# Half of the token projections and of the convolution move from the first block into the gathers' block

## What is computed

```python
xn = rms_norm(h, norm1_g);  proj = xn @ w_in                 # 2560 columns
q, k, v, ga, gg = split(proj)                                # each 512 wide
# 4 heads: differential attention, ALiBi bias, causal, then rms_norm over a head's 128 columns
attn_out = diff_attention(q, k, v, lam, ...)
# 512 channels: u = ga*sigmoid(gg); causal depthwise conv of 31 taps; LayerNorm over groups of 64; silu
conv_out = conformer_conv(ga, gg, conv_w, conv_b, gn_g, gn_b)
h = h + concat([attn_out, conv_out]) @ w_out
# experts: per token 8 heads x top 16 of 128*128 keys; every chosen expert is one row of peer_u and one of peer_v
xn2 = rms_norm(h, norm2_g);  q = xn2 @ wq                    # 8 heads x 256
e, gate = product_key_top16(q, subkeys)
w = gate * gelu(sum_d(u_tab[e] * xn2));   h = h + sum_k(w * v_tab[e])
out = rms_norm(h, final_norm_g)[16:]
```

## Time and profile before

| | us |
|---|---|
| median of 3 runs (3079.91 to 3081.95) | 3081.67 |
| the profiled execution | 3080.33 |
| its span, first to last instruction | 3078.6 |
| mean granted TensorE clock | 0.856 |

### The profile page before, as it was taken

One profiled execution on the slowest core, in us unless ns is written; L12 is line 12 of the kernel. 1 busy time (PEld: TensorE's weight loads), 2 busy tenths in 40 slices (PEclk: granted clock), 3 DMA queues, 4 the chain that ended last, 5 costly groups with the idle time before them and its releaser, 6 DMA issues.

```text
span 3078.6 us, 35490 instructions
## 1 busy us (share of the span) xinstructions
PE 2300.7 (75%) x11776; PEld 848.3 (28%) x11776; DVE 2071.3 (67%) x4903; ACT 1328.8 (43%) x3979; POOL 1162.7 (38%) x1077
## 2 busy tenths in 40 slices
PE   9998857778677777777677777777777777777665
PEld 5555532222222222222222222222222222222211
DVE  3997426666677777777666666666666667666664
ACT  1023523444355555455544444444444444444443
POOL 1001004444354444445444344434444344444442
PEclk9999978898889898889898789878887788887886
DMA  5002139999999999999999999999999999999997
GB/s 215 21 28 73 58 125 415 426 426 427 426 422 426 412 424 416 420 415 426 427 421 426 426 427 426 426 427 423 422 426 425 424 423 425 427 427 421 424 426 310
DMA packets 165608, 1139.68 MB, mean 370 GB/s; under 512 B 18608, under 2 KB 21040, under 8 KB 32688
## 3 DMA queue, kind: packets, MB, share of 16 engines
q0 software_dynamic: 150096, 1082.80, 83.9%
q1 hardware_dynamic: 15328, 54.62, 4.6%
HBM read 1122.06 MB, written 15.28 MB: 369 GB/s over the span
## 4 chain that ended last, share of the span: by engine, by line
DMA 43%; PE 23%; ACT 10%; DVE 6%; issue 3%; POOL 1%; SPq 0%; DVEq 0%; POOLq 0%; ACTq 0%
DMA ring<-table,e_odd 21%; DMA ring<-table,e_even 20%; PE acc L1623 14%; PE qq_ps L1597 5%; DVE ring L1426 4%; ACT diag L1191 2%; ACT weight L1184 2%; ACT L1258 2%; ACT L1177 1%; PE proj L1570 1%; ACT gelu L1258 1%; ACT wide L1215 1%; PE acc L1661 1%; DVE wide L1441 1%; PE s_ps L1614 1%
## 5 line engine op out<-in xcount | busy, mean ns | idle before, releaser
L1623 PE MATMUL acc<-ring,diag 64*64 64x512 f32 x8192 | 1327.4, 734 | 695.0 <-ACT diag L1191 693.3
L1426 DVE CUSTOM_DVE_ANT_0 ring<-ring,xn_odd 128x1024 f32<-128x1024 f32 x512 | 626.7, 1224 | 366.8 <-DMA ring<-table,e_even 183.2
L1040 POOL DMA_INDIRECT ring<-table,e_even x512 | 567.2, 1108 | 791.2 <-PE acc L1623 700.9
L1426 DVE CUSTOM_DVE_ANT_0 ring<-ring,xn_even 128x1024 f32<-128x1024 f32 x512 | 626.4, 1223 | 337.7 <-DMA ring<-table,e_odd 168.7
L1040 POOL DMA_INDIRECT ring<-table,e_odd x512 | 568.1, 1110 | 706.7 <-PE acc L1623 665.3
L1258 ACT ACTIVATE gelu<-dots 128x1 f32<-128x1 f32 x1024 | 205.5, 201 | 1197.0 <-DVE dots L1426 1195.2
L1623 PEld LDWEIGHTS acc<-ring,diag 64*64 64x64 f32 x8192 | 250.0, 150 | 1469.2 <-ACT diag L1191 1342.0
L1191 ACT ACTIVATE diag<-pairs,weight 128x64 f32<-128x64 f32 x1024 | 356.0, 348 | 33.6
L1597 PE MATMUL qq_ps<-wq_rest,xnT_cur 128*128 128x256 f32 x896 | 262.6, 430 | 0.0
L1597 PEld LDWEIGHTS qq_ps<-wq_rest,xnT_cur 128*128 128x128 f32 x896 | 173.1, 209 | 174.1 <-issue 154.0
L1184 ACT ACTIVATE weight<-gelu,gate_even 128x1 f32<-128x1 f32 x512 | 150.7, 294 | 16.7
(11 more groups left out here) (237 smaller groups left out, 2106.3 us busy)
## 6 DMA issues: line engine op xcount, KB each, us to landing
ring<-table,e_even POOLq DMA_INDIRECT x512, 15.1
ring<-table,e_odd POOLq DMA_INDIRECT x512, 15.1
wq_rest<-wq SPq DMA_DIRECT2D x7, 1024.0 KB, 13.0
w_own<-w_units SPq DMA_DIRECT2D x10, 512.0 KB, 3.4
xT<-xt SPq DMA_DIRECT2D x8, 520.0 KB, 7.6
h_next<-x SPq DMA_DIRECT2D x8, 512.0 KB, 8.1
wide<-w_out SPq DMA_DIRECT2D x2, 2048.0 KB, 8.5
wide<-w_out SPq DMA_DIRECT2D x1, 4096.0 KB, 17.5
```

The costliest lines, as they stand in the source:

```text
L1040: pool.indirect_dma_start(out=ring[:, g % RING, :], out_offset=None, in_=table[:, :], in_offset=bass.IndirectOffsetOnAxis(ap=e_row[m % 2][ ...
L1426: dve.tensor_tensor_reduce(ring[:, g % RING, 0:D], ring[:, g % RING, 0:D], xn[(m // PH) % 2][:], 1.0, 0.0, ALU.mult, ALU.add, dots[:, k:k ...
L1623: ins = pe.matmul(acc[ACC_OF[t]][ROWS[j], HALF[i]], diag[ROWS[i], g % DIAGS, :], ring[ROWS[i], g % RING, D + j * 512:D + (j + 1) * 512], s ...
```

## The change

The first block now projects and convolves only the first 528 positions (`FRONT`: meta tokens and early tiles), in two segments of 264. The other 512 positions stay as raw transposed tokens in `x2`, normalised in the first block (`normalise_late`). Their projections become 20 jobs in the gathers' block, one a step from frame -7 (`FIRST_JOB`) to 12: SP loads the job's 512 KB of weights into the one buffer `w_job`, PE makes it in eight pieces in slots 6 to 13, ACT (for A units DVE) takes it out of PSUM in slot 14, SP stores keys, queries and values. The convolution of 512 tokens of one channel unit follows its A job: one tap a slot for 31 slots, then mean, variance, root, four part reciprocals, product, silu, store. Group means' matrix and the last 30 convolution inputs of the early half go through DRAM. Late attention moves back by 32 slots (`FRAME0` = 174), the order of output projections becomes 2, 3, 1, 4. Two pairs of expert heads (4, 5 and 6, 7) share two query-weight buffers: six reloads of 1 MB (`next_pair`), and from step 24 heads 4 and 5 lie in what was `x2` (two more). The first normalisation waits for `g2_row` alone.

```diff
-SEGS = [(0, 352), (352, 352), (704, 336)]
+FRONT = META + P * EARLY
+BACK = P * LATE
+SEGS = [(0, FRONT // 2), (FRONT // 2, FRONT // 2)]
...
-        FILLERS = [(Q[1], 0), (Q[1], 1), (K[2], 0), (K[2], 1), (K[2], 2), (Q[2], 0), (Q[2], 1), (K[3], 0), (K[3], 1),
-                   (K[3], 2), (Q[3], 0), (Q[3], 1), (Q[1], 2), (Q[2], 2), (Q[3], 2)]
+        FILLERS = [(Q[1], 0), (Q[1], 1), (Q[2], 0), (Q[2], 1), (K[3], 0), (K[3], 1), (Q[3], 0), (Q[3], 1)]
...
+            def normalise_late():
+                dve.wait_ge(p_std, 3)
+                dve.reciprocal(rstd[:, FRONT:POS], rstd[:, FRONT:POS]).then_inc(p_rstd, 1)
+                dve.wait_ge(p_rstd, 2)
+                for k in range(KC):
+                    dve.scalar_tensor_tensor(out=x2[:, k, :], in0=x2[:, k, :], scalar=g1_cols[:, k:k + 1],
+                                             in1=rstd[:, FRONT:POS], op0=ALU.mult, op1=ALU.mult).then_inc(p_xn, 1)
...
             gated(1)
-            taps(1, 0, 20)
-            centre(0, 0)
-            centre(0, 1)
-            taps(1, 20, TAPS)
+            taps(1, 0, 8)
+            normalise_late()
+            centre(0)
+            taps(1, 8, 16)
             divide(0)
+            taps(1, 16, TAPS)
...
+            for k in range(KC, 2 * KC):
+                mean_squares(k)
...
-FRAME0 = (1 * PH + 0) * TOPK + 14
+FRAME0 = (1 * PH + 2) * TOPK + 14
+FIRST_JOB = -7
+JOBS = [K[0], G[0], A[0], Q[0], V[0], K[1], G[1], A[1], Q[1], V[1], K[2], G[2], A[2], Q[2], V[2], K[3], Q[3], V[3], G[3],
+        A[3]]
+PIECES = {6: (0,), 7: (1, 2), 8: (3,), 9: (4, 5), 11: (6,), 13: (7,)}
+ORDER = [2, 3, 1, 4, 5, 6, 7]
...
+        def conv_at(m, k):
+            g = TOPK * m + k - FRAME0
+            for c in range(CG):
+                at = g - TOPK * (JOB_AT[A[c]] + 1)
+                if -2 <= at < 4 * TOPK:
+                    return c, at
+            return 0, -9
...
+            def job_weights(n):
+                sp.wait_ge(j_pe, n)
+                sp.dma_start(w_job, w_units[JOBS[n]]).then_inc(j_w, 16)
+
+            def job_store(n):
+                j = JOBS[n]
+                sp.wait_ge(j_ev, n + 1)
...
+                sp.dma_start(dst, kept[:]).then_inc(j_st, 16)
...
+            def next_pair(t, pair):
+                sp.wait_ge(b_q, PH * t + 5 + pair)
+                sp.dma_start(wq_rest[:, 3 + pair], wq[HEAD_ORDER[t % 2][6 + pair]]).then_inc(b_wq[3 + pair], 16)
...
+            def job_out(n):
+                j = JOBS[n]
+                act.wait_ge(j_pe, n + 1)
...
+                    act.activation(kept[:], src, ACT.Copy).then_inc(j_ev, 1)
...
-            dve.wait_ge(b_par, 48)
+            dve.wait_ge(b_g2, 16)
             normalise(0)
...
+                    c, at = conv_at(m, k)
+                    if at == -2:
+                        gated(c)
+                    elif 0 <= at < TAPS:
+                        tap(c, at)
+                    elif at == 39:
+                        centre(c)
+                    elif 43 <= at < 47:
+                        inverse(c, at - 43)
+                    elif at == 47:
+                        divide(c)
...
+            def tap(c, i):
...
+                    dve.scalar_tensor_tensor(out=y[:], in0=u_back[:, i:i + BACK], scalar=cpar[:, i:i + 1], in1=y[:],
+                                             op0=ALU.mult, op1=ALU.add).then_inc(c_dve, 1)
...
+            def job_piece(n, k):
+                j, f = JOBS[n], FIRST_JOB + n
+                if k == 0:
+                    pe.wait_ge(j_w, 16 * (n + 1))
+                    if n >= 1:
+                        pe.wait_ge(j_ev, n)
+                    if 0 <= f < UNITS:
+                        pe.wait_ge(t_z, sc_at[f + 1])
+                    elif FRAME0 + TOPK * f + 6 >= PH * TOPK:
+                        pe.wait_ge(b_acc, 2)
...
+                    ins = pe.matmul(job_banks(f), w_job[:, k, :], x2[:, k, :], start=(k == 0), stop=(k == KC - 1))
```

More of the change, by code:

```diff
@@ L582, in _ @@
             dve.tensor_scalar(sub_gain[:], par[:, KC:KC + 1], 1.0 - LAM_INIT, None, ALU.mult).then_inc(p_lam, 1)
-            dve.wait_ge(p_lamv, 16)
+            dve.wait_ge(p_std, 2)
+            dve.reciprocal(rstd[:, 0:FRONT], rstd[:, 0:FRONT]).then_inc(p_rstd, 1)
+            dve.wait_ge(p_rstd, 1)
+            for n in range(2):
+                raw_keys(0, n)
+            for k in range(KC):
+                normalise(k)
+            for n in range(2):
+                raw_keys(1, n)
+            dve.wait_ge(p_par, 32)
             for n in range(2):
@@ L673, in raw_unit @@
                 w_s = slot(K[h])
-                for n in range(2, -1, -1) if h == 1 and k == 0 else range(3):
+                for n in range(2):
                     lo, w = SEGS[n]
-                    if h == 1 and k == 0 and n == 0:
-                        pe.wait_ge(p_std, 1)
                     ins = pe.matmul(seg_bank(K[h], n)[:, 0:w], w_s[:, k, :], xT[:, k, lo:lo + w], start=(k == 0),
@@ L923, in expert_phase @@
         sc_ps = [acc[0][:, 0:512], acc[0][:, 512:D]]
+        mean_ps = acc[0][:, 512:D]
         b_const = sem("b_const")
-        b_par = sem("b_par")
-        b_wq = [sem(f"b_wq{h}") for h in range(PH)]
+        b_g2 = sem("b_g2")
+        b_gf = sem("b_gf")
+        b_wq = [sem(f"b_wq{h}") for h in range(1, PH)]
         b_w2 = sem("b_w2")
@@ L1113, in _ @@
[L1113 to L1128 removed]
+            sp.dma_start(group_mean, dram["group_mean"]).then_inc(t_bias, 16)
@@ new lines, in _ @@
+            conv_inputs(0)
+            for f in range(FIRST_JOB, UNITS + 1):
+                n = f - FIRST_JOB
+                for c in range(CG):
+                    if f == JOB_AT[A[c]] + 4:
+                        conv_store(c)
+                        if c + 1 < CG:
+                            conv_inputs(c + 1)
+                if f == -3:
+                    sp.wait_ge(b_hin, 2)
+                    fetch(2)
+                    keys_and_queries(0)
+                elif f == -2:
+                    values(0)
+                elif f in (-1, 0, 7, 8):
+                    next_pair(1 if f < 1 else 2, (f + 1) % 8)
+                elif f == 5:
+                    sp.wait_ge(b_hin, 3)
+                    fetch(3)
+                elif f == 13:
+                    sp.wait_ge(j_pe, len(JOBS))
+                    for pair in range(2):
+                        sp.dma_start(wq_last[:, pair], wq[4 + pair]).then_inc(b_wq[5 + pair], 16)
+                    sp.wait_ge(b_hin, 4)
+                    tokens(4)
+                if f == UNITS:
+                    sp.wait_ge(c_st, 16 * CG)
+                    sp.wait_ge(t_pv, UNITS)
+                    sp.wait_ge(t_o, UNITS)
+                    sp.dma_start(w_out_s, w_out).then_inc(b_w2, 16)
+                if f >= 0 and f % LATE == LATE - 1 and f + 1 < UNITS:
+                    keys_and_queries(f // LATE + 1)
+                if f >= LATE and f % LATE == 0:
+                    keep_head(f // LATE - 1)
+                if n + 1 < len(JOBS):
+                    job_weights(n + 1)
+                if n < len(JOBS) and JOBS[n] in KEPT:
+                    job_store(n)
+                if f >= 0 and f % LATE == LATE - 1 and f + 1 < UNITS:
+                    values(f // LATE + 1)
+                if f in (-2, 6, 14):
+                    store((f + 2) // 8)
```

706 lines of the change are left out of this document (420 added, 286 removed).

## The result

The kernel after takes 3063.9 us (median of 6 runs, 3061.6 to 3071.4); the kernel before, run beside it on the same chip, 3081.4 (3079.0 to 3085.4). The ratio is 0.9946, with a 95% interval of 0.9933 to 0.9958: faster by 17.5 us, where 61 were forecast, and 6 us outside the range of 2990 to 3058, among the times (3060 to 3087) that had got a chance of 0.04.

The account below looks back on a forecast made before the run. Before the first gather PE, DVE or their chain bounds, afterwards the full DMA transfers. From 3080.3 us, minus 130.3 for an earlier first gather, plus 57 for bytes, plus 12 for engines: 3019 us, range 2990 to 3058.

Parts of the forecast that it names:

- To the first tap: First block, start to first convolution tap: fewer and shorter PE matmuls bring it from 83.41 to 47.6 us, gain 35.8.
- First tap to first early score: First block's next stage, 172.0 us before: shorter taps and divisions, less new work and waits, gain 42.
- Early attention: First block's early attention loop: PE and DVE lose segment work, 136.5 us becomes 104, gain 32.
- Block start: Second block's start to first gather: DVE no longer waits for `gf_half`, first normalisation at 4.9 instead of 24.6 us; gain 20.5.
- (d): Early attention bound by its chain, first means waited for longer: front gain 95 instead of 130, 3054 us; chance 0.08.
- (e): At the second block's start something else holds the first normalisation: 20 us less gain, 3039 us; chance 0.07.
- The bytes: Behind the first gather: 23.3 MB added cost 57 us (54 to 61), none hidden while DMA is full.
- Do the engines keep up?: Gathers' part with attention: added DVE and PE work mostly fits the slack; 12 us lost, between 0 and 40.
- (c): Slower than before: 5.6 us more waiting in each of 16 attention steps uses up the gain; at 7, 3102 us; chance 0.06.
- `wide <- acc` doubled: Sign that the forecast is wrong: `wide <- acc` waits double.
- Rival (a): Engines never show, DMA stays full at each step, only the bytes come back: 3007 us, down to 2994; chance 0.22.
- (b): DVE becomes the bound through the attention steps, 25 to 45 us over DMA's time: 3035 to 3055 us; chance 0.17.

Follow-up runs that it names:

- gf_only: Kernel before with one edit: the second block's first normalisation waits only for the g2 row, the final-gain wait moves to the first final scale; 3061.6 us, ratio 0.9937.
- thin_both: Kernel after with one of eight matmuls per projection bank and taps on 8 columns instead of 512 in the gathers' part; 3016.9 us, ratio 0.9786.
- the late loads: Kernel after plus 40 unused loads of 262 KB (10.5 MB) in the steps behind the attention; 3091.0 us, ratio 1.0035.
- thin_loads: Kernel after with 19 of 20 job weights loaded with only 8 of 1024 columns, 9.9 MB less; 3059.7 us, ratio 0.9925.
- thin_taps: Kernel after with each convolution tap of the gathers' part on 8 columns instead of 512; 3063.2 us, ratio 0.9943.
- scores_ahead: Kernel after with attention scores issued ahead of the combination in PE's slots 0, 2 and 4, instead of behind it; 3020.7 us, ratio 0.9798.
- thin_jobs: Kernel after with PE making one of eight matmuls of each projection bank in the gathers' part; 3026.5 us, ratio 0.9819.

## Why the prediction was wrong, step by step

**To the first tap**: 45.6 for 47.6, gain 37.8 for 35.8. Right.

**First tap to first early score**: 136.7 us for 129.5, gain 35 for 42. The wait for the first means was 17.00, as said. The third `centre` waited 11.96 for its store, where I took 2.5: ACT did the silu only behind the evictions of Q0 and K2. A mis-sized term, 7 us with the rest.

**Early attention**: 182.28 to 284.97, 102.7 for 104. **Tail** 25.2 for 24.2. **Block start** 25.7 for 25, gain 19.7 for 20.5, shown alone by `gf_only`. Rivals (d) and (e) are out. The sum, 125.7 for 130.3, is right.

**The bytes**: 57 held, as `thin_both` (59 with what little engine loss is left) and the late loads show. Summed over the stretches, 1123.0 MB move behind the first gather, 1099.7 before: the 23.3 that were counted. The sign "23 MB more in all" was put wrongly: the page's total grows by 17.1 (1156.82 against 1139.68 MB), since the first block moves less. That none of it is hidden was wrong in the attention steps (`thin_loads`), but only because the engines were worse there.

**Do the engines keep up?** This step failed: 12 us taken, 0 to 40 allowed, some 51 measured. The part of it that was wrong is how much longer DVE would wait for the other engines: 0 to 3.5 us a step were allowed, 5.6 measured. (A step is 16 gathers, and the kernel's `NSTEPS` is 8 tiles x 8 heads = 64, not the 128 named at the start.)

The sum of DVE's slack was sound, even cautious. By the counts of dot products (239 in 620 us before, which are 14.9 steps and not the 15.3 I had, and 252 in 740 after) a step went from 41.5 to 47.0 us. DVE's busy time grew by 4.5 a step where 98 / 16 = 6.1 were taken, 0.7 of waits among them, and its waits for gathers fell by 4.5, from 4.8 to 0.3: that slack absorbed its own work whole. `thin_taps` says the same from the other side.

What broke was the bound on PE's lateness: that PE "comes later to the scores of the next unit", and DVE waits longer for these scores and for what else it takes from PE, I bounded at 3.5 us a step and then placed near its lower end "since PE's own slack is the larger". DVE's waits for other engines, all groups, grew from 6.2 to 11.8 us a step, just the 5.6 that rival (c) named. The sign I had set for it, `wide <- acc` doubled, did not show: the waits for the attention's scores (L1888) grew only from 4.5 to 6.2. New were 1.8 a step for `gated`, `centre` and `divide` (L1666, L1682, L1688), and the waits for the routing's scores grew by 0.7 (L1529) and those around the heads' norms and outputs by 1.3 (L1647, L1651, L1660). Most of these belong to the same turn of the engines: `scores_ahead` moved only the attention's scores, and took 78 us off their waits and some 30 off the others. It took away old waits too, 4.5 a step that the kernel before had under its transfers.

PE's 164.6 us of waits for the diagonal were no slack to spend. PE stood for ACT, ACT for DVE, and DVE for PE's scores: the idle time of each is a part of the same turn. A job piece on PE in one slot lengthens the turn there, and PE's idle time in another slot can't pay it back, since nothing on PE may run ahead of its program order. PE's waits for the diagonal fell only from 11.0 to 9.2 us a step (145.0 in 740 us, 164.6 in 620), with some 7 us a step more of work on it.

(c) had the size of the waits, and yet the kernel came out faster: it reckoned DVE's slack as almost spent (17 of 115 us left), where 115 - 16 x 4.5 = 43 were. 16 x 5.6 - 43 = 47, near the 51 measured. Rival (a), that the engines never show, is what `thin_both` and nearly `scores_ahead` are. (b) came near the amount (25 to 45 over the transfers' time) with the wrong culprit, DVE instead of PE's order.

The Trainium skill, page "Perfetto Trace Analysis", section "Optimization Strategies", says that when the matmul engine idles for others one should "optimize those engines that are blocking the critical path". Here the row names ACT's diagonal, behind it stands DVE, and a lighter DVE gave nothing (`thin_taps`). What gave 43 us (`scores_ahead`) was to follow the wait around until it comes back, and to cut the link that only program order makes.

What I should have asked of the earlier trace rows is not how large the slack is, but what 67.4 us of waits for scores were made of. The queries and the combination in front of them were there in the kernel before, and an order that puts anything more on PE was bound to lengthen them.

Still open: what makes up the 14 us by which `scores_ahead` stays below the full rate in its attention steps (417 of 425 GB/s), and why `thin_loads` gave 4 to 6 us where the seven loads ahead of the attention alone should give 8.6; its interval allows both.

## What to carry to other kernels

Idle time of an engine counts as slack only if the engine can reach later work during it. In a loop where engines wait for each other in turn, find the operation that another engine waits for and ask what stands ahead of it in program order without being needed by it; put it first before adding work to that engine. And split a composite change before judging it: here one moved wait was worth as much as the whole, and the rest gave some 106 us in front and took 110 behind.

## What was not expected of the hardware

PE's granted clock in the attention steps was no lower with the added matmuls: a mean of 0.90 in the kernel after and 0.92 in `scores_ahead`, against 0.89 before; where PE had least to do it was lower, 0.86 in `thin_jobs` and 0.88 in `thin_both`. The added matmuls still cost more than the 0.434 us of the first block:

```profile
L1939 PE MATMUL acc<-x,wide 128*128 128x512 f32 x146 | 87.6, 708 | 0.0
```

87.6 / 146 = 0.60 us of busy time for each, 9.6 for a job of 16, where 6.9 to 9 were taken. A single one lasts 0.59 us in the first block too; only where many follow each other and overlap does it come to 0.434. So a part is the short runs in which the pieces stand; how much the clock adds, no run here separates. What sets the clock between its two levels, 1.2 and 2.4 GHz, no run here tells.

Added loads by the sync engine cost 24 to 27 us for 10.5 MB when DMA is full, 2.3 to 2.6 us a MB; 425 GB/s would be 2.35, and the share of q1 (7.2% of 3087.2 us for 86.28 MB) says 2.6, as in the earlier trace rows. The two ends can't be told apart.
